# Half of each gate's tiles made as pairs of seven block products between V and the heads

## The reference

```
h = x @ w_in      -> diff-attn q, k, v | window q, k, v | gates g_a, g_b (1024 columns each)
A = differential attention (8 heads, chunk-causal, rotary; the samples see a cache of 512 rows)
B = sliding-window attention (16 q heads, 2 kv heads, rotary, learned sinks)
x = LayerNorm(ALPHA * x + (sigmoid(g_a) * (A @ w_branch_a) + sigmoid(g_b) * (B @ w_branch_b)) @ w_o)
x = LayerNorm(ALPHA * x + relu(x @ w_up) ** 2 @ w_down)
```

## Time and profile before

| | |
|---|---|
| median of 3 runs | 2213.12 us (2213.08 to 2213.55) |
| the profiled execution's own time | 2212.84 us |
| its span, first to last instruction | 2211.1 us |
| granted clock, mean | 0.999 |
| PE busy | 2201.1 us, 100% of the span |
| PEld busy | 2009.0 us, 91% |
| DVE busy | 1267.3 us, 57% |
| ACT busy | 1046.9 us, 47% |
| DMA | 247.19 MB, mean 112 GB/s |

### The profile page before, as it was taken

How to read it: one execution, slowest core, us unless ns; L and a number is a source line. 1 busy time by engine, 2 the same in 40 slices (tenths; PEclk the granted TensorE clock), 3 DMA queues, 4 the chain that set the end, 5 groups by cost and what they waited for, 6 DMA issues and landing times.

```text
span 2211.1 us, 38058 instructions
## 1 busy us (share of the span) xinstructions
PE 2201.1 (100%) x15481; PEld 2009.0 (91%) x15485; DVE 1267.3 (57%) x2105; ACT 1046.9 (47%) x2204; POOL 0.2 (0%) x4
## 2 busy tenths in 40 slices
PE   9999999999999999999999999999999999999998
PEld 7888899999989898989888888999999898989897
DVE  5477752475366663736645777524743665736466
ACT  3477751585223353626225777516842232626261
POOL 0000000000000000000000000000000000000000
PEclk9999999999999999999999999999999999999999
DMA  6555522212231222222255555222132312222222
GB/s 260 219 201 197 203 79 75 64 59 106 77 124 39 77 77 86 86 77 86 105 189 192 191 203 203 72 74 72 49 115 74 118 44 81 79 84 87 67 104 78
DMA packets 58348, 247.19 MB, mean 112 GB/s; under 512 B 10008, under 2 KB 10904, under 8 KB 53792
## 3 DMA queue, kind: packets, MB, share of 16 engines
q1 hardware_dynamic: 42848, 152.75, 20.0%
q10 hardware_dynamic: 15328, 92.02, 11.5%
HBM read 228.49 MB, written 18.09 MB: 112 GB/s over the span
## 4 chain that ended last, share of the span: by engine, by line
PE 99%; DVE 0%; DMA 0%; issue 0%; DVEq 0%; ACT 0%
PE PS L516 14%; PE PS L518 14%; PE PS L517 14%; PE PS L591 10%; PE PS L589 10%; PE PS L590 10%; PE PS L532 4%; PE PS L530 4%; PE PS L531 4%; PE PS L716 2%; PE PS L741 2%; PE PS L680 1%; PE PS L631 1%; PE PS L843 1%; PE PS L730 1%; PE PS L824 1%
## 5 line engine op out<-in xcount | busy, mean ns | idle before, releaser
L516 PE MATMUL PS<-xt_hi,w_hi 128*128 128x320 f32 x1568 | 499.7, 319 | 0.0
L1702 DVE TENSOR_TENSOR w_lo<-w_raw,w_hi 128x1024 fp32r<-128x1024 f32 x226 | 274.7, 1223 | 375.9 <-ACT w_hi L1082 372.4
L518 PE MATMUL PS<-xt_hi,w_lo 128*128 128x320 f32 x1568 | 484.4, 309 | 0.0
L517 PE MATMUL PS<-xt_lo,w_hi 128*128 128x320 f32 x1568 | 484.2, 309 | 0.0
L1082 ACT ACTIVATE w_hi<-w_raw 128x1024 fp32r<-128x1024 f32 x226 | 237.2, 1058 | 484.0 <-PE PS L591 315.9
L589 PE MATMUL PS<-w_hi,act_a_hi 128*128 128x512 f32 x800 | 312.2, 390 | 0.0
L591 PE MATMUL PS<-w_hi,act_a_lo 128*128 128x512 f32 x800 | 311.4, 389 | 0.0
L590 PE MATMUL PS<-w_lo,act_a_hi 128*128 128x512 f32 x800 | 311.4, 389 | 0.0
L516 PEld LDWEIGHTS PS<-xt_hi,w_hi 128*128 128x128 f32 x1568 | 294.7, 188 | 11.0 <-ACT rope_s L1109 7.6
L517 PEld LDWEIGHTS PS<-xt_lo,w_hi 128*128 128x128 f32 x1568 | 295.0, 188 | 0.2
L518 PEld LDWEIGHTS PS<-xt_hi,w_lo 128*128 128x128 f32 x1568 | 294.3, 188 | 0.0
(11 more groups left out here) (252 smaller groups left out, 3702.4 us busy)
## 6 DMA issues: line engine op xcount, KB each, us to landing
w_raw<-in_weights SPq DMA_DIRECT2D x274, 512.0 KB, 3.5
kc<-in_k_cache ACTq DMA_DIRECT2D x16, 2048.0 KB, 8.4
vc<-in_v_cache ACTq DMA_DIRECT2D x16, 2048.0 KB, 8.5
v_out<-rows ACTq DMA_DIRECT2D x2, 2560.0 KB, 8.7
k_out<-k_t ACTq DMA_DIRECT2D x16, 320.0 KB, 2.4
x_t<-in_x_cols SPq DMA_DIRECT2D x8, 320.0 KB, 6.4
rows<-in_x_rows ACTq DMA_DIRECT2D x1, 2560.0 KB, 11.9
x_all<-rows ACTq DMA_DIRECT2D x1, 2560.0 KB, 10.9
```

Source lines behind the costliest of these rows:

```text
L516: mm(out, wh, hi[:, k, c], start=(k == 0), stop=False)
L517: mm(out, wh, lo[:, k, c], start=False, stop=False)
L518: last = mm(out, wl, hi[:, k, c], start=False, stop=(k == KT - 1))
L1702: v.tensor_tensor(w_lo[slot][:], raw[:, raw_of(s, n)[0], :], w_hi[slot][:].bitcast(F32), ALU.subtract)\
```

## The change

In each layer tiles 4 to 7 of g_a and of g_b, eight tiles, are no longer made in the branches but as four combined pairs between V and the heads. `x_sums` now runs twice a layer, the first time in the stretch of V. The raw gates (before the Sigmoid) go to `tmp1` and `tmp2`, are stored to a new tensor in memory, `gates_kept`, by ACT's queue (two stores of 320 KB a pair), and are loaded back in the branches (`load_gate`), where ACT applies the Sigmoid (`kept_gate`). `kc` and `vc` of head 0 are loaded in the last pair and behind it, since the sums of x lie in their place; `v_out` is stored behind the first pair. Before head 0, ACT and DVE wait for all eight stores of the layer. The other gate tiles are as before. The weight stream is reordered to match, `z_all` moves to another region, and the last four tiles of x at the start share two semaphores.

```diff
-V_CHUNKS, HEAD_CHUNKS, BRANCH_CHUNKS, O_CHUNKS = 8, 2 * HEADS, 2 * KT, 8
+V_CHUNKS, GATE_CHUNKS, HEAD_CHUNKS, BRANCH_CHUNKS, O_CHUNKS = 8, 8, 2 * HEADS, KT + 4, 8
...
-AT_HEADS = AT_V + V_CHUNKS - 2
+AT_GATES = AT_V + V_CHUNKS
+AT_HEADS = AT_GATES + GATE_CHUNKS - 2
...
                     row_group(nth(l, AT_V) + 2 * v, l * GROUPS + v, xt_hi, xt_lo,
                               before_bank=lambda r: r == RT - 1 and rope_pair_free(l * ROPES + 1), banks=V_BANKS)
 
+                rope_pair_free(l * ROPES + 2)
+                for u in range(FF_PAIRS):
+                    combined_pair(*pair_at(l, 0, u), 8 * l if u == 0 else None)
+                pe.wait_ge(c11_taken, pair_at(l, 0, FF_PAIRS)[0])
+
                 all_heads(pe, l, head)
...
+                for f in range(KT):
+                    if f == 2:
+                        pe.wait_ge(gate_ready, l * 16 + 4)
+                    else:
+                        pe.wait_ge(branch_taken, l * 16 + (f if f < 2 else f - 1))
                     product_a(f)
                     if f == 0:
                         pe.wait_ge(gate_copied, 6 * l + 3)
-                    else:
-                        pe.wait_ge(gate_ready, l * 16 + f + 3)
-                    feature_tile(0, nth(l, AT_BRANCH_A, gate_chunk(3)[1]) + f, xt_hi, xt_lo, 0)
-                for f in range(KT - 3, KT):
-                    s, i = a_chunk(f)
-                    if a_pair(f) == 0:
-                        pe.wait_ge(gate_ready, l * 16 + KT)
-                    else:
-                        pe.wait_ge(branch_taken, l * 16 + (KT - 3 if f < KT - 1 else KT - 2))
-                    product_a(f)
...
                     else:
                         product_b(f, n)
-                    if f < KT - 4:
-                        s, i = gate_b_chunk(f + 4)
-                        pe.wait_ge(gate_ready, l * 16 + 8 + f + 4)
-                        feature_tile(s, nth(l, AT_BRANCH_B, i), xt_hi, xt_lo, 0)
 
...
                     if f < 4:
-                        s, i = gate_b_chunk(f + 4)
-                        act.wait_ge(chunk_done[s], nth(l, AT_BRANCH_B, i) + 1)
-                        fn(halves(gate_b_of[f][:]), pair(0), ACT.Sigmoid).then_inc(gate_ready, 1)
-                        high(s, nth(l, AT_BRANCH_B, i + 1))
+                        load_gate(gate_b_of[f][:], l, 1, f + 4)
+                    if 0 < f < 5:
+                        kept_gate(gate_b_of[f - 1][:], l, 1, f + 3)
...
+                if u == 0:
+                    act.wait_ge(rope_added, l * ROPES + 2)
+                else:
+                    act.wait_ge(gate_stored, 16 * (KT * l + 2 * u))
+                if odd:
+                    act.wait_ge(chunk_done[1], n + 1)
+                    fn(tile, up_bank(X5), ACT.Copy).then_inc(c21_taken, 1)
+                else:
+                    act.wait_ge(chunk_half_done[0], n + 1)
+                    fn(tile, up_bank(X1), ACT.Copy).then_inc(c11_taken, 1)
...
+            def keep_gates(l, u):
+                q, n = pair_at(l, 0, u)
+                act.wait_ge(up_taken, 2 * q + 2)
+                act.wait_ge(c11_taken, q + 1)
+                act.wait_ge(c21_taken, q + 1)
+                for odd, tile in ((0, tmp1), (1, tmp2)):
+                    act.dma_start(gates_kept[l, u // 2, 2 * (u % 2) + odd], tile[:]).then_inc(gate_stored, 16)
...
+            def gate_pair(l, u):
+
+                last = u == FF_PAIRS - 1
+                n = pair_at(l, 0, u)[1]
+                if u > 0:
+                    gate_half(l, u - 1, 1)
+                    part_highs(l, 0, u, (6,))
+                up_seed(l, 0, u, 0)
+                if u > 0:
+                    keep_gates(l, u - 1)
+                if last:
+                    part_highs(l, 0, u, (4,))
+                else:
+                    part_highs(l, 0, u + 1, (0,))
+                up_fifth(l, 0, u)
+                if not last:
+                    part_highs(l, 0, u + 1, (1,))
+                else:
+                    high(0, nth(l, AT_HEADS, 1), skipped=1)
+                up_seed(l, 0, u, 1)
+                if not last:
+                    part_highs(l, 0, u + 1, (2,))
+                else:
+                    act.wait_ge(up_done, 3 * pair_at(l, 0, u)[0] + 3)
+                    load_cache(0, l, 0)
+                gate_half(l, u, 0)
+                if not last:
+                    part_highs(l, 0, u + 1, (3,))
+                up_seed(l, 0, u, 2)
+                if not last:
+                    part_highs(l, 0, u + 1, (5,) if u + 1 == FF_PAIRS - 1 else (4, 5))
+                else:
+                    gate_half(l, u, 1)
+                    load_cache(1, l, 0)
+                    keep_gates(l, u)
+                    high(1, nth(l, AT_HEADS, 1))
+
+            def load_gate(tile, l, branch, f):
+                act.dma_start(tile, gates_kept[l, branch, f - 4]).then_inc(gate_loaded[f % 2], 16)
+
+            def kept_gate(tile, l, branch, f):
+                act.wait_ge(gate_loaded[f % 2], 16 * (4 * l + 2 * branch + (f - 4) // 2 + 1))
+                fn(tile, tile, ACT.Sigmoid).then_inc(gate_ready, 1)
...
-                load_cache(0, l, 0)
-                load_cache(1, l, 0)
-                for v in range(0, 2):
-                    group_high(nth(l, AT_V) + 2 * v)
-
-                for r in range(RT):
-                    act.wait_ge(row_evacuated[r], l * GROUPS + 2)
-                act.dma_start(v_out[l], rows[:]).then_inc(v_stored, 16)
+                group_high(nth(l, AT_V))
+                t_high(l, 0, 1)
+                high(0, nth(l, AT_V, 3))
+                t_high(l, 0, 2)
+                t_high(l, 0, 3)
+                high(1, nth(l, AT_V, 3))
+                t_high(l, 0, 4)
+                part_highs(l, 0, 0, range(7))
+                for u in range(FF_PAIRS):
+                    gate_pair(l, u)
+                    if u == 0:
+                        for r in range(RT):
+                            act.wait_ge(row_evacuated[r], l * GROUPS + 2)
+                        act.dma_start(v_out[l], rows[:]).then_inc(v_stored, 16)
                 act.preload_act_table_set("natural_log_exp_and_others")
+                wait_apart(act, gate_stored, 16 * KT * (l + 1))
                 all_heads(act, l, head)
...
                 if l:
                     wait_apart(dve, y_stored, 16 * l)
-                for half in range(0, 2):
-                    take_group(l * GROUPS + half, nth(l, AT_V) + 2 * half + 2, half, banks=V_BANKS)
+                n = nth(l, AT_V)
+                for s in range(2):
+                    low(s, n + 1)
+                x_sums(l, 0, 1)
+                low(0, n + 2)
+                for r in range(RT):
+                    take(l * GROUPS, n + 2, r, half_rows(0)(r), None, V_BANKS)
+                low(1, n + 2)
+                x_sums(l, 0, 2)
+                low(0, n + 3)
+                x_sums(l, 0, 3)
+                if l:
+                    dve.wait_ge(input_rows, l * ROW_STEPS)
+                first_pair_weights(l, 0)
+                x_sum_low(l, 0, 4)
+                for r in range(RT):
+                    take(l * GROUPS + 1, n + 4, r, half_rows(1)(r), None, V_BANKS)
+                part_low(l, 0, 0, 5)
+                part_low(l, 0, 0, 6)
+                for u in range(FF_PAIRS):
+                    gate_pair(l, u)
+                wait_apart(dve, gate_stored, 16 * KT * (l + 1))
                 all_heads(dve, l, head)
```

More of the change, by code:

```diff
@@ L93, in build @@
 def build(nc, x_rows, x_cols, k_cache, v_cache, swa_kc, swa_vc, swa_k_keep, swa_v_keep, weights, cols,
-          lam_vec, ln_par, cos_t, sin_t, ident_d, ones_d, masks, x_all, k_out, v_out, swk_out,
+          lam_vec, ln_par, cos_t, sin_t, ident_d, ones_d, masks, gates_kept, x_all, k_out, v_out, swk_out,
           swv_out, swk_keep_out, swv_keep_out):
@@ L343, in build @@
         p5_copied, c21_taken = sem("p5_copied"), sem("c21_taken")
+        gate_stored, gate_loaded = sem("gate_stored"), [sem(f"gate_loaded{i}") for i in range(2)]
         pair_hi_made = sem("pair_hi_made")
@@ L420, in part_place @@
         def part_place(n, o):
-            return 0 if o == 4 and (n - AT_FF // 2) % (CHUNKS // 2) % 8 == FF_PAIRS - 1 else o
+            i = n % (CHUNKS // 2)
+            last = (i - AT_FF // 2) % 8 == FF_PAIRS - 1 if i >= AT_FF // 2 else i == AT_GATES // 2 + FF_PAIRS - 1
+            return 0 if o == 4 and last else o
         def norm_tile(l, which, r):
@@ L1454, in up_seed @@
                     act.wait_ge(chunk_done[0], n + 1)
+                    if u == 0 and part == 0:
+                        act.wait_ge(row_evacuated[4], l * GROUPS + 2)
                     if q:
@@ L2043, in half_rows, with x_sums @@
                 return lambda r: rows[:, r, bass.ts(h, BANK)]
-            def x_sums(l, u):
+            def x_sums(l, which, u):
+                before = 8 * l + 4 * which
                 hi, lo = [[[quarter(t[:].bitcast(F32), k, r) for r in range(2)] for k in range(2)]
```

(69 more changed lines are left out.)

137 lines of the change are left out of this document (77 added, 60 removed).

## The result

| | before | changed |
|---|---|---|
| median, five runs each | 2213.27 us (2213.08 to 2213.55) | 2235.45 us (2235.07 to 2237.77) |
| ratio, 95% interval | | 1.0103 (1.0091 to 1.0114) |
| span of the profiled execution | 2211.1 us | 2235.0 us |
| granted clock, mean | 0.999 | 0.992 |
| DMA | 247.19 MB | 257.69 MB |

The forecast was 2219.0 us, at most 2226. The direction was right, the size was not: 22.2 us over the median of before, where 6 were expected.

A forecast was written before the change was run, and what follows sets the result against it. PE was taken as the bound, with 99% of the span. Waits and clock of 10.15 us per layer, 20.3 in two, less 14.1 saved, give +6.2 on 2212.8: 2219.0 us; own range about 2214 to 2224, wider range 2204 to 2226.

The forecast's parts named there:

- Removed matmuls: On PE, 96 fewer matmuls of 320 columns in both layers, all on the path: 14.1 us saved.
- DVE's and ACT's additions at nothing: In V, the pairs and the branches, added DVE and ACT work is covered by PE and costs nothing.
- The cover of `kc`: At head 0, `kc` lands before PE wants it, covered by 1.5 us.
- Pair 1: At product 6 of pair 1, PE waits for pair 0's gate stores behind `v_out`: 1.4 us (0.8 to 2.1).
- Head 0: In head 0, the last gate stores land behind `vc`, so PE waits 6.35 us for `dec_exp` (5.15 to 6.95).
- The clock: After head 0's wait PE runs slowly, as at the start: 2.4 us per layer.
- Nothing after the short one: After pair 1's short wait, no slow-clock cost was forecast.
- Rival C: The waits come as forecast but without the clock's share: 2214.2 us; chance 0.2.
- A: Gate stores do not wait behind the load, so pair 1 and head 0 have no wait: 2198.7 us; chance 0.15.
- B: Stores land when `vc` is about half done: 3 us wait a layer, no clock loss, 2204.7 us; chance 0.05.
- D: More waits: first pair's row copies 1.5 us late, `kc` up to 2 us, each layer: +7, about 2226; chance 0.1.

The follow-up runs named there:

- all three repairs: Changed kernel with `v_out` stored at the end of head 0, last pair's gate stores ahead of `vc`, two copies issued with chunk 32: 2199.57 us, 0.9940 of before.
- experiment 4: Changed kernel plus 33 unread matmuls of 512 columns ahead of head 0's `unit_score` in each layer: 2230.19 us, 1.0078 of the kernel before.

## Why the prediction was wrong

- **Removed matmuls, 14.1 us: right.** The run with all three repairs has 13.6 us less span than before and no new wait.
- **DVE's and ACT's additions at nothing: right.** No wait on row copies, sums or kept gates appears in the changed kernel or the repaired one. The cover of `kc` was thinner than said: it landed at 138.2 (issued at 128.69, 9.5 us), and PE asked at 139.1. That is 0.9 us, not 1.5, and with the stores by GpSimd it was gone (3.4 us of waits).
- ***Pair 1*, 1.4 us a layer: the largest miss, 7.7 and 3.5.** The step that failed is "for the two stores of a pair behind something large I take 2.4 us". `v_out` itself landed as forecast (9.0 us). The stores landed 9.3 us behind it in layer 0 and 5.2 in layer 1. Its bounds came from ACT's queue alone; here weight loads and, in layer 0, 1792 KB of copies ran on SP's queue beside them. That chunk 16 would be loaded earlier follows from the new order of the stream; I moved the weight chunks and did not look at what is tied to their numbers. The upper bound of 3.1 us was also too low by its own numbers: 2.5 us for the first store and half of 1.8 us for the second make 3.4. Without the copies layer 0's wait was 3.2 us, so they made 4.5 us of it.
- ***Head 0*, 6.35 us a layer: the mechanism right, 1.5 us short.** The stores landed 2.7 and 2.5 us behind `vc`, as said (2.4). `vc` took 9.9 and 10.5 us in place of 8.5: a median over sixteen heads was used for a place in which `kc` is still under way (it landed 2.4 us after `vc` was issued) and weight loads too. That this overlap is what makes `vc` slower was not tested by itself.
- ***The clock*, 2.4 us behind each long wait: that PE is slow there was right; for head 0 the size was right in sum by chance** (1.6 and 3.0). The 2.4 us and the spacing of 0.28 us are the author's estimates from one slow stretch, the start: 11 matmuls of 512 columns in 4.87 us, 443 ns each, against 227 ns in V. No run shows that term as such, nor that the start is slow for the same reason as the stretches behind the waits: ahead of it the trace has 1.55 us of idleness, not several, and the granted clock reads 1.00 over it, where it reads 0.50 behind the waits. What the runs show in place of the 2.4 us is starts 0.267 us apart and stretches of 0.1 to 3.0 us behind waits of 3.1 us or more, of very different cost behind waits of much the same length. "Nothing after the short one" failed: pair 1's waits were 7.7 and 3.5 us, not 1.4, and cost 2.8 us more each. Rival C, no clock share, is refuted by the spacing of 0.267 us and by experiment 4.
- **Rivals A and B.** Their condition, stores landing well ahead of `vc`, did not come about: 148.4 against 145.7. D's size was passed, but by none of its mechanisms.

By terms: the waits were forecast at 15.5 us and were 26.9 (11.4 short: pair 1 short by 8.4, head 0 by 3.0); the clock at 4.8 and what is left for it was 11.1 (6.3 short). Together 17.7 us, and the profiled execution, 2236.77 us, is 17.8 over the forecast.

## What to carry to other kernels

A store on which the next step waits is issued ahead of the large transfer that can wait, in the order of the program. In these runs the queue it is on did not help (9.0 and 11.3 us beside `vc` on GpSimd's, 10.2 and 11.7 on ACT's), the order of issue did (2.9 and 3.3 us ahead of `vc`). When a stream is reordered, look for everything that is tied to its chunk numbers, and see beside what it now falls. A wait of PE had a price beyond its length here, the slow clock behind it: waits of 3.1 us and more cost 0.1 us in one place and 1.5 to 3.0 us in the others. It belongs in a forecast as a range.

## What was not expected of the hardware

- A wait of 3.5 us, in layer 1, had the same slow stretch behind it (24 matmuls in 6.35 us) as the one of 7.7 us in layer 0 (6.34 us). Over all runs the price did not grow with the wait's length: 8.2 us cost 1.5, 3.2 us cost 0.1 in one place and 1.6 in two others. What sets it is open.
- With the stores by GpSimd a wait of only 2.3 us, for `kc` in head 0 of layer 0, was followed by the slow clock: the 16 matmuls behind it took 3.01 us in place of 1.92, and the granted clock read 0.50 in 141 to 143 us.
- The slow stretch in head 0 of layer 0 was half that of layer 1 (1.6 against 3.0 us), behind waits of 7.6 and 8.1 us. What sets this is open.
- `vc` issued behind the two gate stores landed in 12.2 us instead of 9.9, while the stores fell from 10.2 and 11.7 to 2.9 and 3.3 us. The last of the three landed at 148.4 in one case and 148.7 in the other: the order of issue shared out the same time, and PE's wait hung on the stores, not on `vc`.
